# A hybrid decoder layer on one core: projections with the column chunk as the innermost loop, so that consecutive matmuls write three PSUM banks in turn

## The chip, the cores and the metric

The kernel runs on one core of a Trainium2 chip. The metric is the device time of one execution in microseconds (us); lower is better. Before the change the median of three runs is 1958.12 us (1958.08 to 1958.41).

## What is computed

The reference is one inference step of one decoder layer, for a prompt of 1040 tokens (16 meta tokens and 1024 others) and for 8 decode samples of one token each, all in fp32. Cut to what matters here:

```python
xn = rms_norm(x, attn_norm_w)
q, k, v, qi, ki, wi, cx, cb, cc, ga, gc = split(xn @ w_in)        # 1024 -> 5444 features
q, k = rope(rms_norm(q)), rope(rms_norm(k));  qi, ki = rope(qi), rope(ki)
attn = attend(q, k, v, qi, wi, ki)          # top-256 keys by an indexer, then softmax over them
u_hist = concat([conv_prev, cc * cx]);  conv_out = cb * causal_dwconv(u_hist, conv_w)
mixed = sigmoid(ga) * (attn @ w_o_attn) + sigmoid(gc) * (conv_out @ w_o_conv)
h = x + mixed @ w_merge
g, val = split(rms_norm(h, ffn_norm_w) @ w_up)                     # 1024 -> 2 * 2816
y = h + (silu(causal_dwconv(concat([ffn_prev, g]), ffn_conv_w) + b) * val) @ w_down
```

## The kernel before, in words

All tokens stand side by side as columns: 1040 prompt tokens, 8 decode tokens and 8 columns of padding make TP = 1056, cut into NCH = 3 column chunks of CH = 352. Features lie on the 128 partitions, so an activation of 1024 features is 8 feature blocks (KD = 8) of 128 x 1056.

**The projections** (x @ w_in, attn @ w_o_attn, conv_out @ w_o_conv, mixed @ w_merge, hn @ w_up) are done in tiles of 128 output features. Both operands of such a product are split into a high and a low fp32r part: SyncE loads the weights of a tile into WRAW (512 KB), ScalarE casts them to WHI (`hi`, line 899), GpSimd computes WLO = WRAW - WHI (`lo`, line 1301); XH and XL are the same two parts of the activation (AH, AL for the attention output, COH, COL for the convolution's). TensorE computes a tile as WHI * XH + WHI * XL + WLO * XH, over 8 feature blocks: 3 chunks x 8 blocks x 3 operand pairs = 72 matmuls, each with a stationary 128x128 block and 352 moving columns. A tile accumulates in PS[b], a tensor of three PSUM banks, one bank for each column chunk; b alternates between 0 and 1 from tile to tile, as do the weight buffers. A last matmul raises mm[b]; ScalarE or VectorE then reads all three banks at once and frees PS[b] through ps_free (or f_g, f_a, h_out, o_m0, o_m1, by stage).

Where these tiles are computed:

- `proj` (line 469): 42 tiles of x @ w_in. Nine calls of it carry a function `mid`, which was called between the first column chunk and the second, that is behind 24 of the 72 matmuls: `head_weights` (line 513, nine small transposes whose result ScalarE copies to WI at line 961) once, and `head_sums` (line 584, three matmuls that sum the squares of a head into PX, awaited by ScalarE through r_ms before it writes SELC, line 1019, and SQ again) eight times.
- `out_part` (line 780): 8 output tiles, each in two parts of 36 matmuls (4 feature blocks), one for the attention output into PS[0] and one for the convolution's into PS[1].
- `plain` (line 824): 7 tiles of the merge product and 43 of the up projection.
- `first_proj` (line 497) and the first merge tile (line 834) already run over the feature blocks outermost, because the blocks come in one by one; there the column chunk is the middle loop and the operand pair the innermost, so the PSUM bank changes behind every third matmul. They are not touched.

The down projection (`down`, line 857), the attention (lines 659 to 759) and the indexer (line 554) are not touched either. In the indexer a unit of matmuls has one stationary block, QS[h], and runs over 512-column chunks of the keys; each chunk has its own bank and gets two matmuls, one with KH2 and one with KL2.

The order of the work on each engine is the order of the code; loops with `Fori` are loops of the chip's sequencers.

Of the kernel before, what the change touches and what calls it, by code (L numbers as in the profile page):

```python
# [31 lines left out]
KD = D // P  # L32
# [5 lines left out]
NCH = 3  # L38
# [47 lines left out]
def build(nc, io):  # L86
    ctx = ExitStack()
    with ctx:
# [3 lines left out]
        def at(name, shape, off, dt=F32):  # L92
            n = 4
            for s in shape[1:]:
                n *= s
            assert base + off + n <= nc.sbuf_usable_end, (name, off, n)
            return nc.alloc_sbuf_tensor_at(name, shape, dt, offset=base + off)
# [5 lines left out]
        WHI = [at(f"WHI{b}", [P, KD, P], 8192 + 4096 * b, F32R) for b in range(2)]  # L103
        WLO = [at(f"WLO{b}", [P, KD, P], 16384 + 4096 * b, F32R) for b in range(2)]
# [40 lines left out]
        XH = at("XH", [P, KD, TP], o7, F32R)  # L145
        XL = at("XL", [P, KD, TP], o7 + 8 * R, F32R)
# [35 lines left out]
        AH = at("AH", [P, 4, TP], o1, F32R)  # L182
        AL = at("AL", [P, 4, TP], o1 + 4 * R, F32R)
        COH = at("COH", [P, 4, TP], o2, F32R)
        COL = at("COL", [P, 4, TP], o2 + 4 * R, F32R)
# [272 lines left out]
        def _(pe):  # L458
            def proj(b, k, xh, xl, mid=None, extra=None, kn=KD):

                pe.wait_ge(w_lo[b], k + 1)
                if not (isinstance(k, int) and k == 0):
                    pe.wait_ge(ps_free[b], k)
                if extra:
                    extra()
                for c in range(NCH):
                    for kk in range(kn):
                        for p, (w, x) in enumerate(((WHI, xh), (WHI, xl), (WLO, xh))):
                            last = nc.tensor.matmul(PS[b][:, c, 0:CH], w[b][:, kk, :], x[:, kk, c * CH:(c + 1) * CH],  # L469
                                                    start=(kk == 0 and p == 0), stop=(kk == kn - 1 and p == 2))  # L470
                    if c == 0 and mid:
                        mid()
                last.then_inc(mm[b], 1)

# [29 lines left out]

            first_proj(0, 0, 0)
            proj(1, 0, XH, XL, extra=lambda: pe.wait_ge(n_t, 8))

            def head_weights():
# [6 lines left out]
                last.then_inc(wi_t, 1)  # L515

            proj(0, 1, XH, XL, head_weights)


# [23 lines left out]
            for b in range(2, NB):  # L543
                for h in range(IH):
# [6 lines left out]
                    for c0 in range(0, S_W[b], 512):  # L551
                        w = min(512, S_W[b] - c0)
# [27 lines left out]
            def head_sums(j, b, ready):  # L580
# [6 lines left out]
                return go  # L587

            proj(1, 1, XH, XL, extra=lambda: pe.wait_ge(s8_c, 1))
            proj(0, 2, XH, XL, head_sums(0, 1, 2))  # L590
            with pe.Fori(1, 4) as i:
# [181 lines left out]
            attend(3, True, decode_values)  # L773

            def out_part(b, q):
                for c in range(NCH):
                    for kk in range(4):
                        xh, xl = ((AH, AL), (COH, COL))[q]
                        for p, (w, x) in enumerate(((WHI, xh), (WHI, xl), (WLO, xh))):
                            last = nc.tensor.matmul(PS[q][:, c, 0:CH], w[b][:, 4 * q + kk, :], x[:, kk, c * CH:(c + 1) * CH],  # L780
                                                    start=(kk == 0 and p == 0), stop=(kk == 3 and p == 2))
                return last

            def outs(b, k, m):
                pe.wait_ge(w_lo[b], k + 1)
                for q in range(2):
                    pe.wait_ge((o_m0, o_m1)[q], m)
                    out_part(b, q).then_inc(mm[b] if q else o_ps, 1)
# [3 lines left out]
            for t in range(NB):  # L792
                if t >= 4:
                    pe.wait_ge(at_l, t - 3)
                for j in range(4):
                    last = nc.tensor.transpose(at_banks[t % 4][:, j * P:j * P + ROWS[t]], AT[0:ROWS[t], t, j * P:(j + 1) * P],
                                               CK[0:ROWS[t], C_ID:C_ID + ROWS[t]])
                last.then_inc(at_t, 1)
                if t == 3:
                    pe.wait_ge(d_o, 2)  # L800
                    for j in range(4):
                        last = nc.tensor.matmul(PS[0][:, 1, 8 * j:8 * j + 8], OD[:, j * P:(j + 1) * P], CK[0:64, C_OH:C_OH + 8],
                                                start=True, stop=True)
                    last.then_inc(d_at, 1)
                    pe.wait_ge(co_l, 3)
                    pe.wait_ge(co_lp, 1)
                    pe.wait_ge(w_lo[1], 22)
                    out_part(1, 1)
            pe.wait_ge(at_l, NB + 1)
            out_part(1, 0).then_inc(mm[1], 1)  # L810
            outs(0, 22, 1)
            with pe.Fori(1, 4) as i:
# [4 lines left out]
            def plain(b, k, wait):  # L817

                pe.wait_ge(w_lo[b], k + 1)
                wait()  # L820
                for c in range(NCH):
                    for kk in range(KD):
                        for p, (w, x) in enumerate(((WHI, XH), (WHI, XL), (WLO, XH))):
                            last = nc.tensor.matmul(PS[b][:, c, 0:CH], w[b][:, kk, :], x[:, kk, c * CH:(c + 1) * CH],  # L824
                                                    start=(kk == 0 and p == 0), stop=(kk == KD - 1 and p == 2))
                last.then_inc(mm[b], 1)
# [3 lines left out]
            for kk in range(KD):  # L830
                pe.wait_ge(o_lo, kk + 1)
                for c in range(NCH):
                    for p, (w, x) in enumerate(((WHI, XH), (WHI, XL), (WLO, XH))):
                        last = nc.tensor.matmul(PS[1][:, c, 0:CH], w[1][:, kk, :], x[:, kk, c * CH:(c + 1) * CH],
                                                start=(kk == 0 and p == 0), stop=(kk == KD - 1 and p == 2))
            last.then_inc(mm[1], 1)
            plain(0, 26, lambda: pe.wait_ge(o_m0, 8))
            with pe.Fori(1, 4) as i:
                plain(1, 25 + i, lambda: pe.wait_ge(h_out, 2 * i - 1))
                plain(0, 26 + i, lambda: pe.wait_ge(h_out, 2 * i))  # L840
# [1056 lines left out]
```

## Time and profile before

| | before |
|---|---|
| median of 3 runs | 1958.12 us (1958.08 to 1958.41) |
| span of the profiled execution (first to last instruction) | 1953.8 us |
| mean granted TensorE clock over the span | 0.953 |
| PE busy, weight loads busy | 1825.9 us (93%), 1731.0 us (89%) |
| VectorE, ScalarE, GpSimd busy | 53%, 30%, 31% |
| matmul records, weight-load records | 11067, 11067 |

The page gives the span of the profiled execution and no other time of it; the median of the three runs is 4.3 us above that span, which holds what lies around it. PE is TensorE's matmuls and PEld its weight loads, which run beside the matmuls. Each matmul record is some 320 ns long while a new one starts about every 160 ns, so the costs are read from the starts and not from the durations. The granted clock is given as a share of full speed: 1.00 is 2.4 GHz and 0.50 is 1.2 GHz.

### The profile page before, as it was taken

The page shows a single profiled execution, that of the slowest core. Times are in us where ns is not written, and L with a number is a line of the kernel's source. Part 1 is how long each engine was busy: PE and PEld are TensorE (multiplying, and loading weights), DVE is VectorE, ACT ScalarE, POOL GpSimd, SP SyncE. Part 2 cuts the span into 40 slices and gives each one's busy share as a digit, 9 for nine tenths or more (in the row PEclk, how much of TensorE's full clock was granted, in tenths as well). Part 3 has the DMA queues.
Part 4 walks back from the last instruction along what each step waited for, and adds up shares of the span by engine and source line. Part 5 has one row for each costly group of instructions (what it writes and reads, how often), then busy time and mean ns, then how long its engine had stood idle before and what let it go on. Part 6 is the DMA issues. An engine that isn't in the chain of part 4 may idle for free.

```text
span 1953.8 us, 29797 instructions
## 1 busy us (share of the span) xinstructions
PE 1825.9 (93%) x11067; PEld 1731.0 (89%) x11067; DVE 1030.2 (53%) x1716; ACT 589.3 (30%) x812; POOL 603.9 (31%) x278
## 2 busy tenths in 40 slices
PE   4689999999999768899899998999999999999998
PEld 4559996999999767677799988999999999999998
DVE  5469989999940367344444125434433443443443
ACT  4545532232221445344321114121221122113110
POOL 3305744445112488311122214221132122212220
PEclk9789996999999877799999999999999999999999
DMA  4111112112222544234433212111111111111102
GB/s 179 38 61 33 33 54 100 54 54 85 91 91 83 173 129 127 69 109 130 143 110 132 89 54 87 44 51 48 32 55 44 40 54 43 43 43 54 43 11 94
DMA packets 57592, 146.77 MB, mean 75 GB/s; under 512 B 14506, under 2 KB 14634, under 8 KB 57258
## 3 DMA queue, kind: packets, MB, share of 16 engines
q1 hardware_dynamic: 53170, 130.43, 20.7%
q10 hardware_dynamic: 3632, 11.12, 1.5%
q0 software_dynamic: 720, 4.33, 0.6%
q8 instruction: 38, 0.62, 0.1%
q14 instruction: 32, 0.26, 0.0%
HBM read 125.97 MB, written 19.99 MB: 75 GB/s over the span
## 4 chain that ended last, share of the span: by engine, by line
PE 87%; DVE 4%; ACT 3%; POOL 3%; issue 2%; DMA 1%; SPq 1%; DVEq 0%; POOLq 0%; ACTq 0%
PE PS L824 30%; PE PS L469 24%; PE PX L857 13%; PE PS L780 5%; PE PS L759 3%; PE PS L689 3%; PE PS L659 2%; PE PX L672 2%; PE PS L624 1%; PE PS L554 1%; POOL RING L1415 1%; POOL HKL L1396 1%; PE PS L497 1%; DMA RING<-cache_k 1%; ACT ROT L926 1%
## 5 line engine op out<-in xcount | busy, mean ns | idle before, releaser
L1301 POOL TENSOR_TENSOR WLO<-WRAW,WHI 128x1024 fp32r<-128x1024 f32 x103 | 257.2, 2497 | 747.8 <-ACT WHI L899 747.7
L824 PE MATMUL PS<-XL,WHI 128*128 128x352 f32 x1200 | 387.3, 323 | 0.0
L824 PE MATMUL PS<-XH,WLO 128*128 128x352 f32 x1200 | 387.1, 323 | 0.0
L824 PE MATMUL PS<-XH,WHI 128*128 128x352 f32 x1200 | 386.0, 322 | 0.5 <-POOL WLO L1301 0.5
L469 PE MATMUL PS<-XH,WHI 128*128 128x352 f32 x1008 | 327.2, 325 | 3.1 <-DVE S L1565 1.5
L469 PE MATMUL PS<-XL,WHI 128*128 128x352 f32 x1008 | 326.8, 324 | 0.0
L469 PE MATMUL PS<-XH,WLO 128*128 128x352 f32 x1008 | 326.8, 324 | 0.0
L824 PEld LDWEIGHTS PS<-XH,WHI 128*128 128x128 f32 x1200 | 225.4, 188 | 0.8 <-POOL WLO L1301 0.8
L824 PEld LDWEIGHTS PS<-XH,WLO 128*128 128x128 f32 x1200 | 225.4, 188 | 0.0
L824 PEld LDWEIGHTS PS<-XL,WHI 128*128 128x128 f32 x1200 | 225.2, 188 | 0.0
L1581 DVE MATCH_REPLACE8 S<-M,S 128x1024 f32<-128x1024 f32 (+3 forms) x224 | 206.1, 927 | 0.0
L1579 DVE MAX8 M<-S 128x8 f32<-128x1024 f32 (+3 forms) x224 | 201.0, 933 | 1.2
L469 PEld LDWEIGHTS PS<-XH,WHI 128*128 128x128 f32 x1008 | 190.8, 189 | 10.9 <-issue 10.3
L1763 DVE TENSOR_TENSOR XT<-XT,PX 128x352 f32<-128x352 f32 x264 | 137.5, 521 | 112.5 <-PE PX L857 112.5
L469 PEld LDWEIGHTS PS<-XL,WHI 128*128 128x128 f32 x1008 | 190.7, 189 | 0.0
L469 PEld LDWEIGHTS PS<-XH,WLO 128*128 128x128 f32 x1008 | 190.7, 189 | 0.0
L857 PE MATMUL PX<-FH,DHI 128*128 128x352 f32 x528 | 172.1, 326 | 3.7 <-DVE FL L1755 3.7
L857 PE MATMUL PX<-FL,DHI 128*128 128x352 f32 x528 | 170.6, 323 | 0.0
L857 PE MATMUL PX<-FH,DLO 128*128 128x352 f32 x528 | 170.5, 323 | 0.0
L1730 DVE SCALAR_TENSOR_TENSOR TG<-G,WV,TG 128x1056 f32<-128x1056 f32 x22 | 29.0, 1318 | 237.7 <-ACT TG L1259 237.7
L1451 POOL TENSOR_TENSOR DLO<-DRAW,DHI 128x2048 fp32r<-128x2048 f32 x11 | 50.8, 4619 | 225.8 <-ACT DHI L1283 225.8
L899 ACT CAST WHI<-WRAW 128x1024 fp32r<-128x1024 f32 x103 | 107.8, 1046 | 39.2 <-PE PS L824 20.6
(245 smaller groups left out, 2770.3 us busy)
## 6 DMA issues: line engine op xcount, KB each, us to landing
WRAW<-wtiles SPq DMA_DIRECT2D x103, 512.0 KB, 3.5
RING<-cache_k SPq DMA_DIRECT2D x64, 256.0 KB, 3.0
RING<-cache_v SPq DMA_DIRECT2D x64, 256.0 KB, 2.9
DRAW<-wdown SPq DMA_DIRECT2D x11, 1024.0 KB, 4.8
gates<-EV ACTq DMA_DIRECT2D x16, 528.0 KB, 2.7
XT<-xT SPq DMA_DIRECT2D x8, 528.0 KB, 8.0
SGA<-gates SPq DMA_DIRECT2D x8, 528.0 KB, 3.6
SGC<-gates SPq DMA_DIRECT2D x8, 528.0 KB, 4.9
```

What stands on the lines that cost most here:

```text
L469: last = nc.tensor.matmul(PS[b][:, c, 0:CH], w[b][:, kk, :], x[:, kk, c * CH:(c + 1) * CH], start=(kk == 0 and p == 0), stop=(kk == kn - 1 ...
L689: last = nc.tensor.matmul(px_out[u % 2][0:ROWS[b], :], PTB[u % 2][0:w, kt, 0:ROWS[b]], v, start=(kt == 0), stop=(kt == KT_N[b] - 1))
L759: last = nc.tensor.matmul(px_dec[h], PZ[:, (p * NS + smp) * 64:(p * NS + smp + 1) * 64], RING[smp % 2][:, p, h * 256:(h + 1) * 256], start ...
L780: last = nc.tensor.matmul(PS[q][:, c, 0:CH], w[b][:, 4 * q + kk, :], x[:, kk, c * CH:(c + 1) * CH], start=(kk == 0 and p == 0), stop=(kk = ...
L824: last = nc.tensor.matmul(PS[b][:, c, 0:CH], w[b][:, kk, :], x[:, kk, c * CH:(c + 1) * CH], start=(kk == 0 and p == 0), stop=(kk == KD - 1 ...
L857: last = nc.tensor.matmul(PX[q % 2][:, 0:CH], w[:, a, m * P:(m + 1) * P], x[:, a, c * CH:(c + 1) * CH], start=(a == 0 and p == 0), stop=(a ...
L899: nc.scalar.copy(WHI[b][:, :, :], WRAW[b][:, :, :]).then_inc(w_hi[b], 1)
L1301: nc.gpsimd.tensor_tensor(WLO[b][:, :, :], WRAW[b][:, :, :], WHI[b][:, :, :].bitcast(F32), ALU.subtract).then_inc(w_lo[b], 1)
L1451: nc.gpsimd.tensor_tensor(DLO[:, :, :], DRAW[:, :, :], DHI[:, :, :].bitcast(F32), ALU.subtract).then_inc(d_lo, 1)
L1579: ins = nc.vector.max(M8[x][0:ROWS[b], :], s)
L1581: ins = nc.vector.match_replace(s, M8[x][0:ROWS[b], :], s, TAKEN)
L1763: nc.vector.tensor_tensor(h, h, PX[q % 2][:, 0:CH], ALU.add).then_inc(d_px, 1)
```

## The change

In the three functions `proj`, `out_part` and `plain` the loop over the column chunks becomes the innermost one: feature block, then operand pair, then column chunk. Three matmuls in a row now have the same stationary block and write the three banks of PS[b] in turn. `mid` is called behind the third feature block (27 of 72 matmuls). Nothing else changes: the matmuls, their flags on the first and last of each bank, the waits ahead of a tile and the signal behind it are the same.

```diff
@@ proj
-                for c in range(NCH):
-                    for kk in range(kn):
-                        for p, (w, x) in enumerate(((WHI, xh), (WHI, xl), (WLO, xh))):
+                for kk in range(kn):
+                    for p, (w, x) in enumerate(((WHI, xh), (WHI, xl), (WLO, xh))):
+                        for c in range(NCH):
                             last = nc.tensor.matmul(PS[b][:, c, 0:CH], w[b][:, kk, :], x[:, kk, c * CH:(c + 1) * CH],
                                                     start=(kk == 0 and p == 0), stop=(kk == kn - 1 and p == 2))
-                    if c == 0 and mid:
+                    if kk == 2 and mid:
                         mid()
@@ out_part
-                for c in range(NCH):
-                    for kk in range(4):
-                        xh, xl = ((AH, AL), (COH, COL))[q]
-                        for p, (w, x) in enumerate(((WHI, xh), (WHI, xl), (WLO, xh))):
+                for kk in range(4):
+                    xh, xl = ((AH, AL), (COH, COL))[q]
+                    for p, (w, x) in enumerate(((WHI, xh), (WHI, xl), (WLO, xh))):
+                        for c in range(NCH):
@@ plain
-                for c in range(NCH):
-                    for kk in range(KD):
-                        for p, (w, x) in enumerate(((WHI, XH), (WHI, XL), (WLO, XH))):
+                for kk in range(KD):
+                    for p, (w, x) in enumerate(((WHI, XH), (WHI, XL), (WLO, XH))):
+                        for c in range(NCH):
```

Two places show how the instructions move on TensorE; the other engines' instructions are the same, in the same order. The rows give the line, the operation, the output and the two inputs (the activation first, then the stationary block; WHI0 is the buffer of tiles with b = 0), and the output's columns; x3 stands for three such instructions in a row, which differ in the column chunk. Weight loads have no rows of their own: in the trace before, each matmul has one.

The first place is the seam between two up-projection tiles (`plain`, line 824), from a tile in PS0 to one in PS1. Before:

```order
L824 MATMUL PS0<-XH_92,WHI0_51 128x352
L824 MATMUL PS0<-XL_93,WHI0_51 128x352
L824 MATMUL PS0<-XH_92,WLO0_53 128x352
L824 MATMUL PS1<-XH_92,WHI1_52 128x352 [waits f_g,w_lo1]
L824 MATMUL PS1<-XL_93,WHI1_52 128x352
L824 MATMUL PS1<-XH_92,WLO1_54 128x352
```

Now:

```order
L824 MATMUL PS0<-XH_92,WHI0_51 128x352 x3
L824 MATMUL PS0<-XL_93,WHI0_51 128x352 x3
L824 MATMUL PS0<-XH_92,WLO0_53 128x352 x3
L824 MATMUL PS1<-XH_92,WHI1_52 128x352 [waits f_g,w_lo1]
L824 MATMUL PS1<-XH_92,WHI1_52 128x352 x2
L824 MATMUL PS1<-XL_93,WHI1_52 128x352 x3
L824 MATMUL PS1<-XH_92,WLO1_54 128x352 x3
```

The three operand pairs, which came round for every feature block of one chunk, now come once for a feature block, three chunks at a time; the wait ahead of the tile (the bank group is free, the weights are there) stands where it stood.

The second place is `mid` in the one tile that carries `head_weights` (line 513). Before:

```order
L469 MATMUL PS0<-XH_92,WHI0_51 128x352
L469 MATMUL PS0<-XL_93,WHI0_51 128x352
L469 MATMUL PS0<-XH_92,WLO0_53 128x352
L513 MATMUL PX0<-CK_94,EV0_65 128x4 [waits ps_free0]
L513 MATMUL PX0<-CK_94,EV0_65 128x4 x7
L513 MATMUL PX1<-CK_94,EV0_65 32x4
```

Now:

```order
L469 MATMUL PS0<-XH_92,WHI0_51 128x352 x3
L469 MATMUL PS0<-XL_93,WHI0_51 128x352 x3
L469 MATMUL PS0<-XH_92,WLO0_53 128x352 x3
L513 MATMUL PX0<-CK_94,EV0_65 128x4 [waits ps_free0]
L513 MATMUL PX0<-CK_94,EV0_65 128x4 x7
L513 MATMUL PX1<-CK_94,EV0_65 32x4
```

The inserted work stands behind 27 matmuls of the tile instead of 24, and waits for the same semaphore; `head_sums` moves in the same way.

## Rows read from the trace of the kernel before

**Rows 1.** The page: busy time, and the shares of the chain that ended last.

```profile
PE 1825.9 (93%) x11067; PEld 1731.0 (89%) x11067; DVE 1030.2 (53%) x1716; ACT 589.3 (30%) x812; POOL 603.9 (31%) x278
...
PE 87%; DVE 4%; ACT 3%; POOL 3%; issue 2%; DMA 1%; SPq 1%; DVEq 0%; POOLq 0%; ACTq 0%
```

**Rows 2.** Groups by line: matmuls and weight loads of the lines changed.

```profile
L824 PE MATMUL PS<-XL,WHI 128*128 128x352 f32 x1200 | 387.3, 323 | 0.0
L469 PE MATMUL PS<-XL,WHI 128*128 128x352 f32 x1008 | 326.8, 324 | 0.0
L780 PE MATMUL PS<-AL,WHI 128*128 128x352 f32 x96 | 30.8, 321 | 0.0
...
L824 PEld LDWEIGHTS PS<-XL,WHI 128*128 128x128 f32 x1200 | 225.2, 188 | 0.0
```

**Rows 3.** The chain in order of time: start, length (us), what, how many.

```profile
468.22 184.55 PE PS L469 x1152
...
987.90 80.42 PE PS L780 x504
...
1081.46 80.75 PE PS L824 x504
...
1275.38 46.14 PE PS L824 x288
```

**Rows 4.** Timeline of PE, line 834: bank changes behind every third matmul (start, length).

```profile
1069.94 0.32 PE L834 MATMUL PS<-XL,WHI 128*128 128x352 f32 x1
1070.10 0.32 PE L834 MATMUL PS<-XH,WLO 128*128 128x352 f32 x1
1070.26 0.32 PE L834 MATMUL PS<-XH,WHI 128*128 128x352 f32 x1
1070.42 0.32 PE L834 MATMUL PS<-XL,WHI 128*128 128x352 f32 x1
...
1080.97 0.32 PE L834 MATMUL PS<-XL,WHI 128*128 128x352 f32 x1
```

**Rows 5.** Timeline of PE, a line 824 tile: its second matmul and its 71st.

```profile
1194.57 0.32 PE L824 MATMUL PS<-XL,WHI 128*128 128x352 f32 x1
...
1205.62 0.32 PE L824 MATMUL PS<-XL,WHI 128*128 128x352 f32 x1
```

**Rows 6.** Timeline of PE, indexer: one stationary block, bank changes behind every second matmul.

```profile
120.55 0.39 PE L554 MATMUL PS<-KL,QS 128*128 128x512 f32 x1
120.78 0.39 PE L554 MATMUL PS<-KH,QS 128*128 128x512 f32 x1
121.01 0.39 PE L554 MATMUL PS<-KL,QS 128*128 128x512 f32 x1
```

**Rows 7.** Stretches (us): length, PE busy (instructions), granted clock, DMA share, GB/s.

```profile
32.90:37.50 4.60, 4.50 (x15) 0.50 0.41 135
...
1069.70:1081.20 11.50, 11.49 (x72) 1.00 0.50 182
...
1275.40:1321.50 46.10, 46.10 (x289) 1.00 0.17 58
299.00:326.90 27.90, 26.94 (x49) 0.53 0.21 78
```

**Rows 8.** Timeline of PE at the lower clock, line 497.

```profile
33.72 0.49 PE L497 MATMUL PS<-XH,WLO 128*128 128x352 f32 x1
...
37.24 0.49 PE L497 MATMUL PS<-XH,WLO 128*128 128x352 f32 x1
```

**Rows 9.** Timelines of PE and ACT around the two kinds of inserted work.

```profile
62.73 0.68 PE L513 MATMUL PX<-CK,EV 4*128 4x4 f32 x9
...
67.57 0.20 ACT L961 ACTIVATE WI<-PX 128x32 f32<-128x32 f32 x1
...
156.59 1.36 PE L584 MATMUL PX<-SQ,SELC 128*16 128x352 f32 x6
...
153.99 1.06 ACT L1020 ACTIVATE SQ<-PS 128x1056 f32<-128x1056 f32 x1
...
166.89 0.19 ACT L1019 COPY SELC<-CK 128x16 f32<-128x16 f32 x1
```

**Rows 10.** Timeline of PE, line 624: three banks in turn, 16-row operands.

```profile
298.96 2.93 PE L624 MATMUL PS<-RS,SELT 16*128 16x352 f32 x7
```

## The prediction

> **What bounds the kernel now.** I read the page's busy times and its chain first. TensorE is busy for 93% of the span, and 87% of the chain that ended last is matmuls [rows 1]; the other engines are at half or less. So the kernel is a row of matmuls, and the time moves with two things only: the distance from one matmul's start to the next, and the waits between stages. The groups by line come second. They give the number of matmuls that change place: each line has three operand pairs, of which one stands in the rows, so 3 x 1200 on line 824, 3 x 1008 on line 469 and 6 x 96 on line 780 (two parts of three pairs), together 7,200 of the 11,067 [rows 1, 2]. Their mean duration of 322 to 325 ns is no price, because they overlap; nor is the 188 ns of a weight load, which runs beside the matmul ahead of it.
>
> The price is in the chain in order of time. In the long pieces a matmul takes 184.55 us / 1152 = 160.2 ns on line 469, 80.75 / 504 = 160.2 and 46.14 / 288 = 160.2 ns on line 824, and 80.42 / 504 = 159.6 ns on line 780 [rows 3]. These pieces hold four to sixteen tiles each without a gap, so the waits at the seams of tiles are already met when TensorE gets there. The 7,200 matmuls are 7,200 x 160.2 ns = 1,153 us, 59% of the time.
>
> What is in 160.2 ns? At the granted clock of 0.50 (the lower level, 1.2 GHz) twelve matmuls of line 497 start within 37.24 - 33.72 = 3.52 us, 293.3 ns each, which is 352 columns at one a cycle, exactly [rows 7, 8]. At 1.00 (2.4 GHz) the same 352 columns would take 146.7 ns, so 13.3 ns of each matmul are something else. That is what this change could touch; the question is whether those 13.3 ns belong to the stationary block, to the bank, or to neither.
>
> **The change, part by part.**
>
> *The bank changes at every matmul instead of every 24th (every 12th on line 780).* In a tile of 72 there were 3 changes of bank with the seam, and now there are 72: 69 more for each of the 6,624 / 72 = 92 tiles of lines 469 and 824, and 33 more in each of the 16 half tiles of line 780, 6,876 in all. The nearest row is line 834: same operands, same shape, but a new bank behind every third matmul. From its 2nd to its 71st matmul it takes 1080.97 - 1069.94 = 11.03 us [rows 4]; a tile of line 824 takes from its 2nd to its 71st 1205.62 - 1194.57 = 11.05 us [rows 5]. There are 23 changes in the one and 2 in the other. The 21 further changes thus cost -0.02 us, and the four readings, each rounded to 0.01 us, leave about 0.02 us open: between -1.9 and 0 ns a change, with -0.95 ns in the middle. In the four starts around a change, 1070.10 to 1070.26 is no other step than its neighbours [rows 4]. I take 0. As the lower end I keep the middle, 6,876 x 0.95 ns = 6.5 us less. For the upper end no row shows a cost; I bound it by how far two lines of one shape lie apart without a known reason, 160.2 against 159.6 ns [rows 3], with its unrounded 0.65 ns taken as a loss: 7,200 x 0.65 ns = 4.7 us more.
>
> *Three matmuls in a row have the same stationary block; before, two of three did.* This is the point at which one could hope for the 13.3 ns. But the second matmul of each triple (XL with WHI) already follows one with the same block (XH with WHI), and it starts 0.16 us behind it, as the third does with another block [rows 4]. In the indexer all matmuls of a unit have one block, and a bank gets two of them: the step from KL to KH into the next bank is 0.23 us, and so is the step from KH to KL in the same bank [rows 6]. That is the changed order in small, same block and new bank, and nothing is gained. Each of the 11,067 matmuls has its own weight load, also where the block repeats [rows 1, 2], and the change takes no instruction away. Cost: 0.
>
> The Trainium skill ("TensorE: Matmul & The Clock Gate", section "Back-to-back issue gap") gives the distance of isolated warm matmuls as N / 2.4 + 2.5 ns, and its section "Step-by-step: what each phase is for" says that weights may be loaded once for many matmuls. By that an estimate for N = 352 is 149.2 ns, and if the second and third matmul of each block came so, 4,800 x 11 ns = 53 us would go. The trace does not agree for this kernel: matmuls with a repeated block start 160 ns apart [rows 4].
>
> *Inserted work moves by three matmuls (9 tiles), 0.48 us later.* `head_weights` starts at 62.73 and would start at 63.21; its reader, the copy to WI on ScalarE, comes at 67.57, 4 us later, so the delay is covered [rows 9]. `head_sums` starts at 156.59 and lasts 1.36 us; the first instruction of ScalarE that needs it done is the write of SELC at 166.89, so 9 us of cover become 8.5 [rows 9]. A gain is excluded too: the squares that it waits for are ready at 153.99 + 1.06 = 155.05, before TensorE gets there [rows 9]. If the cover were gone, nine delays of 0.48 us would be 4.3 us. Cost: 0.
>
> *Signals and waits of the tiles.* The consumers read all three banks behind the last matmul of the tile, before and after; that banks 0 and 1 were complete earlier was used by nobody. The waits ahead of a tile cover all three banks. The other engines' instructions, and so the queues of SyncE and GpSimd, are unchanged. Cost: 0.
>
> *Sum:* 0 + 0 + 0 + 0. The profiled execution's span of 1953.8 us stays, and with the 4.3 us that the median of the runs lies above it, the time stays at 1958.1 us. With the two ends of the bank's price it is 1951.6 to 1962.8 us.
>
> **The rivals.**
>
> *A repeated block is cheaper when it repeats twice (faster).* If the second and third matmul of a block lost the 13.3 ns, 7,200 x 2/3 x 13.3 ns = 64 us would go: 1894 us. For it: something beside the columns is in the 160.2 ns. Against it: pairs with a repeated block show nothing [rows 4, 6]. Chance 0.04.
>
> *Rotating banks is a little cheaper (faster).* The 0.95 ns a change above, 1951.6 us. For it: 0.02 us between two readings, and the 159.6 ns of line 780, where banks changed twice as often as on line 824 [rows 3 to 5]. Against it: both are at the limit of what can be read. It decides above 0.57 ns a change. Chance 0.08.
>
> *A change of bank costs over a cycle (slower).* The place is the start of each matmul on the three lines, the price 0.65 ns each, 1962.8 us; it decides from 0.54 ns, 3.9 us over 7,200 matmuls. For it: line 834 changes only every third time, and no row shows full-width matmuls that change at each. Against it: 23 changes at no cost [rows 4]. Chance 0.06.
>
> *The clock falls when banks take turns (slower).* The one stretch in which every matmul goes to another of three banks is line 624, and there the granted clock is 0.53, though TensorE is busy for 26.94 of 27.90 us [rows 7, 10]. At that clock 352 columns take 277 ns, 117 ns more than now; over 7,200 matmuls this is 840 us, 2798 us. It decides as soon as 29 of the matmuls run at the lower level, at 133 ns each. Against it: those matmuls have operands of 16 rows only, and line 834, full width with 24 bank changes, runs at 1.00, like line 824 [rows 7]. Chance 0.02.
>
> The Trainium skill has a rule on the side of this last rival ("TensorE: Matmul & The Clock Gate", section "A second HAM failure mode: psum-queue depth-cycling"): a kernel that cycles through PSUM banks in each iteration lets the engine idle for moments, and its clock swings between the two levels. By that rule this change would be a loss. No full-width row here shows it.
>
> **How the numbers follow.** A measurement of this kernel can tell about 0.2%, 3.9 us, from no change. No change has 0.80: the sum rests on pairs and triples that stand in this trace. Faster has 0.04 + 0.08 = 0.12, slower 0.06 + 0.02 = 0.08. The range takes in both ends of the bank's price, 1951.6 and 1962.8, rounded to 1952 and 1963; outside it lie the repeated block and the clock, and a part of the two bank cases.
>
> **What would show it right or wrong.** In the profile after, matmuls and weight loads stay at 11,067 each; the chain's long pieces stay at 160.2 ns a matmul on lines 469 and 824; the granted clock stays at 1.00 in the up projection and near 0.953 over the span; `head_weights` and `head_sums` start 0.48 us later in their tile and nobody waits for them. The forecast is wrong if pieces of line 824 come at 159.6 ns or less or at 160.8 or more, if starts fall into triples of one long and two short steps (the block), if weight loads are fewer, or if the clock of a projection's stretch leaves 1.00.

## The result, and the profile after

| | before | changed |
|---|---|---|
| median | 1958.10 us (1955.02 to 1958.41, 4 runs) | 1968.23 us (1963.05 to 1968.97, 4 runs) |
| ratio to before | 1 | 1.0056 (95% interval 1.0043 to 1.0068) |
| span of the profiled execution | 1953.8 us | 1966.8 us |
| mean granted clock | 0.953 | 0.952 |

The change costs some 10 us: the medians lie 10.1 us apart, and the ratio is put at 1.0056. The forecast was no change, 1958.1 us, with 1963 us as the upper end.

The page after, its line of busy times and its chain by engine (as rows 1 before):

```profile
PE 1836.6 (93%) x11067; PEld 1740.8 (89%) x11067; DVE 1032.3 (52%) x1716; ACT 589.1 (30%) x812; POOL 605.2 (31%) x278
...
PE 87%; POOL 3%; ACT 3%; DVE 3%; issue 2%; DMA 1%; SPq 1%; DVEq 0%; POOLq 0%; ACTq 0%
```

The same number of matmuls and weight loads, no new wait, the same bound; TensorE is busy 10.7 us longer. The chain in order of time (start, length, what, how many) shows where:

```profile
329.75 142.08 PE PS L469 x864
472.26 186.00 PE PS L469 x1152
...
994.98 81.81 PE PS L780 x504
1078.19 11.76 PE PS L834 x72
1089.95 81.37 PE PS L824 x504
...
1261.98 23.10 PE PX L857 x144
1285.07 46.46 PE PS L824 x288
```

Against [rows 3], line 469 went from 184.55 to 186.00 us (160.2 to 161.5 ns a matmul), line 780 from 80.42 to 81.81 us (159.6 to 162.3 ns), line 824 from 46.14 to 46.46 us (160.2 to 161.3 ns). Per tile that is (186.00 - 184.55) / 16 = 0.091 us, (81.81 - 80.42) / 14 = 0.099 us per half tile, and (46.46 - 46.14) / 4 = 0.080 us; times 42 tiles, 16 half tiles and 50 tiles it makes 3.8 + 1.6 + 4.0 = 9.4 us. The untouched lines 834 (11.75 and 11.76 us for 72 matmuls) and 857 (23.09 to 23.15 us for 144, in both) keep theirs. So the loss is some 1 to 3 ns at each of the 7,200 matmuls that the change reorders. The spans of the two profiled executions differ by 3.6 us more, mainly where the clock changes level or TensorE waits (line 624 took 28.00 us in place of 26.92, and from the end of line 469 to the first output tile it took 1.4 us longer); runs of one kernel differ by as much.

The clock is not the reason. Stretches of the kernel after (us; length, PE busy, granted clock, DMA share, GB/s):

```profile
1285.10:1331.50 46.40, 46.40 (x289) 1.00 0.18 57
1078.20:1089.90 11.70, 11.70 (x73) 1.00 0.50 179
470.00:655.00 185.00, 185.00 (x1149) 1.00 0.24 84
```

And the timeline of PE on line 824 of the kernel after, in which three alike matmuls are one row:

```profile
1299.88 0.65 PE L824 MATMUL PS<-XL,WHI 128*128 128x352 f32 x3
1300.37 0.64 PE L824 MATMUL PS<-XH,WLO 128*128 128x352 f32 x3
1300.85 0.65 PE L824 MATMUL PS<-XH,WHI 128*128 128x352 f32 x3
1301.33 0.65 PE L824 MATMUL PS<-XL,WHI 128*128 128x352 f32 x3
```

Three matmuls take 0.48 or 0.49 us from start to start, where 0.48 us stood before. The views print hundredths of a microsecond; the trace's starts have nanoseconds, and below "steps" are the distances between them in ns, the median over the tiles. In the kernel before they repeat from tile to tile, to a nanosecond or so a step and 0.1 ns in the mean of a tile that starts without a wait. With the change they repeat too, except that on line 824 the first tile of each row of tiles has other steps (160.8 to 161.1 ns in the mean; the others 161.5), which is why pieces of four tiles come to 161.3 ns. This regularity is what made the experiments readable. The steps of a line 824 tile, first of the kernel before, then of the change:

```
before  162 159 161 156 160 161 156 161 159 162 162 162 | 162 159 161 156 ...   mean of the tile 160.2
after   161 163 162 164 161 164 159 159 161 163 162 159 162 162 162 164 159 159 | 161 163 ...   161.5
```

### The profile page after: what moved, and what is told of

Its sections match the earlier page's. It is cut to its first block, busy times and chain, and to the rows that moved or that the text cites. A ratio compares the mean times of both kernels' runs of the same rounds, so it can differ in the third digit from the quotient of the medians.

```text
span 1966.8 us, 29797 instructions
## 1 busy us (share of the span) xinstructions
PE 1836.6 (93%) x11067; PEld 1740.8 (89%) x11067; DVE 1032.3 (52%) x1716; ACT 589.1 (30%) x812; POOL 605.2 (31%) x278
## 4 chain that ended last, share of the span: by engine, by line
PE 87%; POOL 3%; ACT 3%; DVE 3%; issue 2%; DMA 1%; SPq 1%; DVEq 0%; POOLq 0%; ACTq 0%
PE PS L824 30%; PE PS L469 24%; PE PX L857 13%; PE PS L780 5%; PE PS L759 3%; PE PS L689 3%; PE PS L659 2%; PE PX L672 2%; PE PS L497 1%; PE PS L624 1%; POOL RING L1415 1%; PE PS L554 1%; DMA RING<-cache_k 1%; POOL HKL L1396 1%; ACT ROT L926 1%
## 5 line engine op out<-in xcount | busy, mean ns | idle before, releaser
L824 PE MATMUL PS<-XL,WHI 128*128 128x352 f32 x1200 | 259.6, 324 | 0.0
L824 PE MATMUL PS<-XH,WHI 128*128 128x352 f32 x1200 | 258.8, 324 | 0.0
L824 PE MATMUL PS<-XH,WLO 128*128 128x352 f32 x1200 | 257.5, 323 | 0.0
L469 PE MATMUL PS<-XH,WHI 128*128 128x352 f32 x1008 | 220.6, 327 | 3.0 <-DVE S L1565 1.5
L469 PE MATMUL PS<-XL,WHI 128*128 128x352 f32 x1008 | 219.8, 326 | 0.0
L469 PE MATMUL PS<-XH,WLO 128*128 128x352 f32 x1008 | 217.5, 324 | 0.0
L824 PEld LDWEIGHTS PS<-XH,WLO 128*128 128x128 f32 x1200 | 205.0, 189 | 0.0
L824 PEld LDWEIGHTS PS<-XL,WHI 128*128 128x128 f32 x1200 | 204.1, 188 | 0.0
L824 PEld LDWEIGHTS PS<-XH,WHI 128*128 128x128 f32 x1200 | 203.8, 188 | 0.3 <-POOL WLO L1301 0.3
L469 PEld LDWEIGHTS PS<-XH,WHI 128*128 128x128 f32 x1008 | 172.1, 190 | 10.8 <-issue 10.3
L469 PEld LDWEIGHTS PS<-XH,WLO 128*128 128x128 f32 x1008 | 173.5, 190 | 0.0
L469 PEld LDWEIGHTS PS<-XL,WHI 128*128 128x128 f32 x1008 | 173.1, 189 | 0.0
```

## The experiments

Three things change from one matmul to the next with the new order: the bank, the stationary block and the moving operand's chunk. Since they are three separate arguments of the instruction, each can be given the new order alone. The chain pieces of line 824 (288 matmuls), line 469 (1152) and line 780 (504) are compared, in us. The ratios are to runs of the kernel before taken beside each, with medians of 1955.4 to 1956.3 us. e1 to e3, e5, e7, e8 and e11 to e13 form other sums than the layer's and serve for their times alone.

| kernel | line 824 x288 | line 469 x1152 | line 780 x504 | ratio to before (95%) |
|---|---|---|---|---|
| before | 46.14 | 184.55 | 80.42 | 1 |
| the change | 46.46 | 186.00 | 81.81 | 1.0056 (1.0043 to 1.0068) |
| e1: banks alone | 46.13 | 184.55 | 80.42 | 0.9999 (0.9989 to 1.0009) |
| e2: moving operand alone | 46.46 | 186.00 | 81.77 | 1.0052 (1.0036 to 1.0069) |
| e3: stationary blocks alone | 46.13 | 184.55 | 80.50 | 0.9997 (0.9987 to 1.0006) |
| e4: before, XH and XL 64 bytes up | 45.81 | 183.17 | 80.42 | 0.9975 (0.9966 to 0.9985) |
| e5: change, chunks 512-byte steps apart | 45.98 | 184.35 | 80.60 | 0.9989 (0.9979 to 0.9998) |
| e6: change, XH and XL 64 bytes up | 46.61 | 186.47 | 81.78 | 1.0050 (1.0033 to 1.0066) |
| e7: one chunk for all | 46.09 | 184.34 | 80.88 | one run, 1955.70 us |
| e8: the same, 64 bytes up | 46.08, 46.40 | 184.34 | 80.88 | one run, 1960.01 us |
| e9: chunk behind every third matmul | 46.08 | 184.34 | 80.32 | 1.0002 (0.9993 to 1.0012) |
| e10: later place of the inserted work alone | 46.13 | 184.55 | 80.42 | 1.0000 (0.9991 to 1.0010) |
| e14: e9, 64 bytes up | 46.08, 45.76 | 183.06 | 81.43 | 0.9987 (0.9977 to 0.9996) |

**e1 to e3: which of the three.** One list of the old order and one of the new, and each argument takes one of them (a function `walk` of ten lines ahead of `proj` moves lines 469, 780 and 824 to 479, 788 and 830):

```diff
+            def walk(kn):
+                slow = [(c, kk, p) for c in range(NCH) for kk in range(kn) for p in range(3)]
+                fast = [(c, kk, p) for kk in range(kn) for p in range(3) for c in range(NCH)]
+                bank, moving, block = fast, slow, slow     # e1;  e2: slow, fast, slow;  e3: slow, slow, fast
```

> The order of before in both operands, but the output goes to the three banks in turn, as in the change (the sums are of other products than the reference's; number, shape and operands of the matmuls are the same). Theory A, a change of bank costs time: in the chain's long pieces lines 469 and 824 of before take 161.3 to 161.5 ns a matmul, as in the change (160.2 before), line 780 takes 162.3 (159.6 before), and the time is about 10 us above before, 1968 us. Rivals, the cost comes from the moving operand, which changes its column chunk at every matmul (B), or from loading one stationary block three times in a row (C): 160.2 and 159.6 ns, 1958 us.

> Banks and stationary blocks in the order of before, but the moving operand in the order of the change, so that its column chunk changes at every matmul (the sums are of other products than the reference's). Theory B, the changing chunk costs time: 161.3 to 161.5 ns a matmul on the projections and 162.3 ns on the output tiles, 1968 us. A (banks) and C (stationary block): 160.2 and 159.6 ns, 1958 us.

> Banks and moving operand in the order of before, but the stationary blocks in the order of the change, each loaded three times in a row (the sums are of other products than the reference's). Theory C, loading a block again costs time: 161.3 to 161.5 and 162.3 ns a matmul, 1968 us. A and B: 160.2 and 159.6 ns, 1958 us.

Chains of e1, e2 and e3, one fence each:

```profile
467.54 184.55 PE PS L479 x1152
990.50 80.42 PE PS L788 x504
...
1276.79 46.13 PE PS L830 x288
```

```profile
470.38 186.00 PE PS L479 x1152
993.41 81.77 PE PS L788 x504
...
1283.40 46.46 PE PS L830 x288
```

```profile
467.68 184.55 PE PS L479 x1152
987.35 80.50 PE PS L788 x504
...
1273.94 46.13 PE PS L830 x288
```

The moving operand's order alone (chunk, feature block, and high or low part, as the change has them) makes the whole loss, with the change's steps to the nanosecond (161.5 ns within a tile on line 469, 161.9 on line 780). A bank change at each of 72 matmuls costs nothing, and a block loaded three times in a row neither costs nor gains anything. Theories A and C fall.

**e4: the 0.6 ns that line 780 was quicker.** In SBUF, as the program allocates it, XH and XL start 64 bytes past a multiple of 128; AH, AL, COH and COL start at a multiple of 128. (These places, and all that follow, are counted from a base that the kernel adds to every offset, a multiple of 32 bytes whose value no run shows.) One edit moves XH, XL and the tensors behind them; of these the matmuls of lines 469 and 824 read XH and XL alone:

```diff
-        o7 = 134080
+        o7 = 134144
```

> The kernel before with XH and all that lies behind it in SBUF moved up by 64 bytes, so that the rows of XH and XL start at a multiple of 128 bytes, as those of AH, AL, COH and COL do. Theory D, a moving chunk that starts 64 bytes off such a multiple costs about 1 ns, which is why line 780 takes 159.6 ns in the chain and lines 469 and 824 take 160.2: lines 469 and 824 fall to 159.1 to 159.6 ns, and 6,624 matmuls give 4 to 7 us, 1951 to 1954 us. Rival, line 780 is quicker for its shorter tiles or for its place: 160.2 ns stay, 1958 us.

Chain of e4:

```profile
467.99 183.17 PE PS L469 x1152
985.61 80.42 PE PS L780 x504
...
1272.19 45.81 PE PS L824 x288
```

Lines 469 and 824 fall to 159.0 and 159.1 ns, line 780 stays. Their tiles now have the steps that line 780 had before (161 162 156 161 155 159). So the place of the moving operand in SBUF bears on the distance between matmuls, and in these long pieces 64 bytes are worth 1.1 to 1.2 ns each. Not every tile gains: the seven pieces of 72 matmuls on line 469 that stand between two `head_sums` take 11.72 to 11.75 us, and took 11.71 before. The median is 1950.20 us against 1955.59 beside it: this is the quickest version here that computes the layer. The kernel before was not as quick as it could be, and its order was not to blame.

**e5: new chunk each time, address unmoved modulo 512 bytes.**

```diff
-    x[:, kk, c * CH:(c + 1) * CH]
+    x[:, kk, (0, 384, 640)[c]:(0, 384, 640)[c] + CH]
```

> The change, but its three chunks of the moving operand start at columns 0, 384 and 640 instead of 0, 352 and 704 (they overlap, so the sums are of other products than the reference's; 352 columns each, as before). These starts are multiples of 512 bytes apart, so that the chunk changes at every matmul and its address modulo 512 does not: it moves 8 times in 72 matmuls, with the feature block, against 72 in the change and 24 in the kernel before. Theory E, what costs is a start address that moves modulo 512; from 161.5 ns with 72 moves and 160.2 with 24, a move is 2.0 ns, and 8 moves give 159.7 ns on the projections; about 1952 us. Rival F, any change of the chunk costs: 161.3 to 161.5 ns stay, 1965 us.

Chain of e5:

```profile
466.73 184.35 PE PS L469 x1152
...
1273.56 45.98 PE PS L824 x288
```

45.98 / 288 = 159.7 ns on line 824 and 184.35 / 1152 = 160.0 on line 469, in place of 161.3 and 161.5. The chunk changes at every matmul and the loss is gone: what costs is the address, not the change of chunk. F falls.

**e6: the change with the shift of e4.**

> The change with XH and XL at a multiple of 128 bytes (64 bytes up). With line 780 as the model, whose operands lie so (159.1 ns within a tile before, 162.0 with the change), theory E gives 162.0 ns on lines 469 and 824: the shift that won 5 us in the order of before loses here, about 4 us above the change, 1969 us. Rival, the shift wins in any order: 160.4 ns, some 7 us below the change, 1958 us.

Chain of e6:

```profile
469.32 186.47 PE PS L469 x1152
...
1281.67 46.61 PE PS L824 x288
```

46.61 / 288 = 161.8 ns and 161.9 within a tile: the same 64 bytes that gain in one order lose in the other, as line 780 had said. The time is level with the change (1966.18 us beside 1956.28 for before), not 4 us above it; 0.5 ns at 6,624 matmuls is 3 us, within what the runs of these two kernels scatter.

**e7 and e8: no move at all.** All matmuls of the three lines read one chunk:

```diff
-    x[:, kk, c * CH:(c + 1) * CH]
+    x[:, 0, 0:CH]
```

> The kernel before, but every matmul of lines 469, 780 and 824 reads the first chunk of the first feature block of its operand (the sums are of other products than the reference's). The start address modulo 512 never moves. Theory E: 160.16 - 24/72 x 2.0 = 159.5 ns on the projections, 157.6 ns on line 780. Rival, the steps are a rhythm of their own: 160.2 and 159.1 ns as before.

> As the run before it, with XH and XL 64 bytes up. From line 780 (159.1 ns with 24 moves in 72, 162.0 with 72) a move is 4.4 ns there, so theory E gives 157.6 ns on all three lines. Rival, the floor does not depend on where the operand lies: 159.5 ns as with the operand unshifted.

Chain of e7:

```profile
469.14 184.34 PE PS L469 x1152
989.15 80.88 PE PS L780 x504
...
1276.05 46.09 PE PS L824 x288
```

Chain of e8:

```profile
469.49 184.34 PE PS L469 x1152
...
1277.58 46.08 PE PS L824 x288
1346.75 46.40 PE PS L824 x288
```

In e7 a matmul takes 160.0 ns in the mean of a tile, on line 780 too, which slowed from 159.1; e8 has the same in the long pieces of lines 469 and 780. Theory E, in which every move has a price, falls: without any move 160.0 ns, and moves can cost (161.5, 161.9) as well as gain (159.0). But on line 824 of e8 only about half of the tiles take 160.0 ns. In the others, 24 of the 49 that start without a wait, always a whole row of tiles behind one another, a matmul takes 161.1 ns (the pieces of 46.40 us), with the same fixed address, the same order and the granted clock at 1.00. So some 1.1 ns can also come with no move at all; see e14.

**e9 and e10: the rest of the change.** e9 swaps the two inner loops of the change (`for c` outside `for p`), e10 is the kernel before with `mid` called three matmuls later.

> The change with its two inner loops swapped: feature block, then column chunk, then operand pair, so that the moving operand's chunk (and the bank) changes behind every third matmul, as on the untouched line 834. Feature block outermost and the later place of the inserted work stay. Theory, only the changing start address at every matmul costs: 160.0 to 160.2 ns on lines 469 and 824, 159 to 160 ns on line 780, no difference from before (within 0.2%). Rival, something else of the nest (the feature block outermost) costs as well: over 160.5 ns and over 1960 us.

> The kernel before with nothing of the change but the place of the inserted work: nine times behind 27 matmuls of a tile instead of 24. Prediction's theory: no cost, within 0.2% of before. Rival: the nine delays are on the path, up to 4.3 us more.

The chain of e9 has, on line 824:

```profile
1275.25 46.08 PE PS L824 x288
```

Both are within 0.1% of before. Feature blocks outermost cost nothing as long as the chunk moves behind every third matmul only, and the later `head_weights` and `head_sums` cost nothing, as the prediction had it.

**e11 to e13: which addresses.** The change again, with other starts of the moving operand, XH and XL 64 bytes up. For line 469, 780 and 824, in this order:

```diff
+    x[:, 0, 64 * c:64 * c + CH]      x[:, 0, 128 * c:128 * c + CH]     x[:, 0, 32 * c:32 * c + CH]          # e11
+    x[:, 0, 16 * c:16 * c + CH]      x[:, 0, 8 * c:8 * c + CH]         x[:, 0, 352 * c:352 * c + CH]        # e12
+    x[:, kk - kk % 2, c * CH:(c + 1) * CH]    x[:, 0, s:s + CH]        x[:, 0, t:t + CH]                    # e13
+    # s = 64 * c + 32 * (kk % 2), t = 32 * c + 32 * (kk % 2)
```

> The change with XH and XL at a multiple of 128 bytes, where all matmuls of the three lines read the first feature block and only the chunk's start moves (the sums are of other products than the reference's): in steps of 64 columns (256 bytes) on line 469, 128 columns (512 bytes) on line 780, 32 columns (128 bytes) on line 824. Fixed starts gave 160.0 ns. Theory G, what matters is the start address modulo 512 bytes: 160.0 ns on line 780, other than 160.0 on lines 469 and 824. Rival H, modulo 256: 160.0 ns on lines 780 and 469, other on line 824. Rival F, any move costs: over 161 ns on all three.

> As the run before it, in steps of 16 columns (64 bytes) on line 469, 8 columns (32 bytes) on line 780, and the change's own 352 columns (1408 bytes, 384 modulo 512) on line 824. Theory G: 161.5 to 162 ns on line 824, as in the change, though the feature block stays; steps of 64 bytes cost too, steps of 32 bytes may. Rival, the cost needs the feature block to move as well: 160.0 ns on line 824.

> The change with XH and XL at a multiple of 128 bytes, and three other ways to walk the moving operand (the sums are of other products than the reference's). Line 469 takes the change's chunks but of even feature blocks only, so that the block moves by multiples of 256 bytes. Line 824 stays in the first feature block and starts at columns 32 c + 32 (kk mod 2), the same addresses modulo 256 bytes as the change has. Line 780 stays there too, at columns 64 c + 32 (kk mod 2). Theory M, the succession of start addresses modulo 256 bytes alone sets the distance: about 160.1 ns on line 469, about 161.9 ns on line 824 as in e6, 159.4 to 160 ns on line 780. Rival, the feature block must move: about 161.9 ns on line 469, 160.1 on line 824.

Chains of e11, e12 and e13 (one run each, 1955.61, 1958.49 and 1962.15 us):

```profile
469.14 184.33 PE PS L469 x1152
988.42 80.88 PE PS L780 x504
...
1275.50 46.09 PE PS L824 x288
```

```profile
471.09 185.19 PE PS L469 x1152
991.50 80.87 PE PS L780 x504
...
1278.33 46.09 PE PS L824 x288
```

```profile
469.06 184.34 PE PS L469 x1152
989.01 80.60 PE PS L780 x504
...
1277.45 46.61 PE PS L824 x288
```

The steps within a tile:

```
e11 780  512-byte steps      160 160 160 160 160 160                                   mean 160.0
e11 469  256-byte steps      160 160 160 160 160 160                                   160.0
e11 824  128-byte steps      165 158 160 160 161 156 | 165 158 ...                     160.0
e12 824  352-column steps    165 158 159 161 161 156 | 165 158 ...                     160.0
e12 469  64-byte steps       161 160 163 159 162 159 163 161 159 | 161 160 ...         160.8
e6  824  the change, shifted 159 164 165 158 161 161 162 162 162 163 165 158 161 161 168 167 159 158   161.9
e13 824  the same modulo 256 159 164 165 158 161 161 162 162 162 163 165 158 161 161 168 167 159 158   161.9
e13 469  even blocks         161 161 156 165 158 159 | 161 161 ...                     160.0
```

The change's 352-column steps behave like steps of 128 bytes (1408 = 5 x 256 + 128), and steps of 256 bytes like none; steps of 32 bytes on line 780 of e12 kept the mean of 160.0 ns as well. On line 824 of e11 theories G and H both expected another mean than 160.0; the single steps changed and the mean did not. In e12 the change's own chunks cost nothing on line 824, against theory G and my number for it. e13 gives the reason: with the blocks moving by multiples of 256 bytes line 469 has no loss either, and line 824, which never leaves the first feature block but has the change's addresses modulo 256 bytes, has its loss, with the same eighteen steps as e6; line 780 came at 159.4 ns within a tile, as M said. Theory M holds here: the same succession of the moving operand's start addresses modulo 256 bytes brings the same steps. It was tried with XH and XL shifted; for the place that they have in the change, e5 with its steps of 512 bytes is all there is. And it is not the whole account: e8 above and e14 below have tiles of different steps for one succession.

It is the succession, not the number of moves. Write a for an address at a multiple of 256 bytes and b for one 128 bytes further. The kernel shifted in e4 reads a a a b b b and takes 159.0 ns; e12 reads a b a a b a and takes 160.0; e6 reads a b a a b a a b a, then b a b b a b b a b, and takes 161.9.

**e14: both edits that do no harm.**

> The order of e9 (feature block, column chunk, operand pair) with XH and XL 64 bytes up. Theory M: within a tile 158.9 ns on all three lines, as line 780 had in e9, so 7,200 matmuls gain 8 us against before: about 1948 us, level with e4 or 1 us better. Rival, the gain of the shift belongs to the order of before alone: 160.0 ns, 1955 us.

Chain of e14:

```profile
467.64 183.06 PE PS L469 x1152
985.63 81.43 PE PS L780 x504
...
1271.98 46.08 PE PS L824 x288
1341.15 45.76 PE PS L824 x288
```

0.9987, half the gain of e4. Line 469 is at 158.9 ns as expected, but tiles whose addresses follow one another in the same way modulo 256 bytes come in three kinds: steps of 161 162 156 161 155 159 (mean 159.0), of 160 161 161 160 157 161 (160.0, 26 of 49 tiles of line 824) and of 159 159 159 164 162 164 (161.2, line 780, which had 158.9 in e9, though its operands and their order are the same in both). So something besides the succession decides, perhaps how a row of tiles was entered: on line 824 here the kind does not change within a row. The order of before, with its shift, is in the quick kind in all its long pieces, and is the better of the two versions.

## Why the prediction was wrong, point by point

- **What bounds the kernel: right.** Matmul starts set the time, and the 7,200 matmuls of the three lines carry the loss.
- **Banks (taken as 0): right.** e1 has 72 bank changes a tile and 160.2 ns. The 0.95 ns a change kept as the lower end was misread: the 0.02 us behind it are in the trace (11,032 ns in line 834's tile, 11,047 in line 824's, a difference that all of its tiles repeat), but they are not the bank's. In e9 line 824 walks its moving operand as line 834 does and has its 160.0 ns.
- **Stationary block (0): right.** e3. Of the 13.3 ns beyond the columns nothing goes with a repeated block; with a fixed moving address they stay, 160.0 - 146.7.
- **Inserted work (0): right.** e10.
- **The step that failed: the list of what changes.** The part on the change priced banks, blocks, inserted work and signals, and asked whether the 13.3 ns belong "to the stationary block, to the bank, or to neither". The third argument of the matmul, whose chunk now also moves at every instruction, had no line in the sum. It was so put at nothing without a reason, and it carries all of the loss (e2): 1.1 to 1.3 ns on lines 469 and 824, 2.8 ns on line 780, 9.4 us in all.
- **Two rows could not have shown it, and were read as if they had.** Line 834 [rows 4] moves its chunk only behind every third matmul, which e9 shows to cost nothing. The indexer [rows 6] was called "the changed order in small"; its chunks lie 512 columns apart, 2048 bytes, a multiple of 256, and of such steps 256 and 512 bytes cost nothing (e11). Its moving address does move, from KH to KL and back, 4224 bytes or 128 past a multiple of 256, but alike at a change of bank and without one, so that the row could not tell the changed order from the old.
- **A row that showed it was put aside.** Line 780 at 159.6 ns beside 160.2 [rows 3] was "without a known reason", and its 0.65 ns became the upper bound. It was the same cause, a moving operand with another start address (e4), and a sign that this argument matters. As a bound it was too small: 9.4 us came, not 4.7.
- **The rival on the slower side** named the start of each matmul on the three lines as the place, rightly, and a price of 0.65 ns, too low; its mechanism, the change of bank, was wrong. The rival of the clock did not come: 1.00 in the stretches above, also with banks in turn.

The rule cited for that rival, the Trainium skill's "A second HAM failure mode: psum-queue depth-cycling" ("TensorE: Matmul & The Clock Gate"), would have the clock swing; no run here shows it, with 72 bank changes a tile in e1 at 160.2 ns and a granted clock of 0.952 over the span, 0.953 before.

What stays open: why a succession of addresses costs or gains. That two kinds of steps occur at one fixed address (e8) and three for one succession (e14) suggests a state that is carried from matmul to matmul; this is not shown, and no run tells which part of the chip would hold it or what sets it.

## What to carry to other kernels

When a loop nest is turned round, list every operand of the instruction and what its address does from one instruction to the next, the moving operand too; look whether the rows used as evidence have the same addresses. For fp32 matmuls of 352 columns, the succession of the moving operand's starts modulo 256 bytes was worth 1 to 3 ns of 160 here: try keeping it for several matmuls in a row, and try a tile's offset in SBUF (64 bytes gave 0.25% here) before changing the order. Differences of one nanosecond between two lines of the same shape are no noise when the steps repeat to the nanosecond; they have a cause not yet found.

## What the runs showed that had not been expected

With a fixed moving address a matmul took 160.0 ns at either place of the operand (e7, e8), but 161.1 in half of the tiles of line 824 in e8. Moves of 256 and 512 bytes left the 160.0 as it is (e11), moves of 128 bytes gave 159.0 to 162.0 ns by their succession, and steps of 64 bytes 160.8 ns (e12). The Trainium skill ("SBUF — State Buffer", section "Specifications (TRN2)") speaks of lines of 16 bytes in SBUF and asks for two hits on a line; by that alone one contiguous fp32 row would be as dear as another, wherever it starts at a multiple of 16 bytes. The runs show more for the moving operand: XH starts at such a multiple in both e4 and before, and 1.1 ns a matmul lie between them.
